# A two-block network on one core: the state space part over groups, its dt chain and the second rotary embedding rewritten

## What is computed

```python
# Mamba-2 mixer: 32 heads of 64, in 8 groups of 4 heads; state 128; 4 chunks of 128 tokens
z, xbc, dt_raw = split(h @ w_in)             # 2048 | 4096 | 32 columns
xbc = silu(causal_conv(xbc) + conv_b)        # -> xs (2048), B (8x128), C (8x128)
dt = softplus(dt_raw + dt_bias);  a = -exp(a_log)
a_cs = cumsum(dt * a)                        # inside each chunk
decay = exp(where(tril, a_cs[l] - a_cs[s], -inf))
y_diag = (C B^T * decay) @ (x * dt)
states = B^T @ (x * dt * exp(a_cs[last] - a_cs));  prev = scan(states, exp(a_cs[last]))
y = y_diag + (C @ prev) * exp(a_cs) + xs * d_skip
y = y * silu(z);  y = y * rsqrt(mean over the group of y^2 + eps) * norm_w
x = x + y @ w_out
# rotary embedding, on the first 32 of 128 dimensions of each head (6 key heads, 24 query heads)
out = concat([x1*cos - x2*sin, x2*cos + x1*sin, rest])     # x1, x2: 16 dimensions each
```

## Time and profile before

| | us |
|---|---|
| three runs: lowest, median, highest | 3761.51, 3762.31, 3772.96 |
| the profiled execution, its own time | 3773.22 |
| its span, first to last instruction | 3771.2 |
| TensorE busy | 3442.8 (91%) |
| VectorE, ScalarE, GpSimd busy | 1583.9, 881.0, 1646.8 |
| mean granted TensorE clock | 0.946 of 2.4 GHz |

### The profile page before, as it was taken

How to read it: one execution, slowest core, us unless ns; L and a number is a source line. 1 busy time by engine, 2 the same in 40 slices (tenths; PEclk the granted TensorE clock), 3 DMA queues, 4 the chain that set the end, 5 groups by cost and what they waited for, 6 DMA issues and landing times.

```text
span 3771.2 us, 43722 instructions
## 1 busy us (share of the span) xinstructions
PE 3442.8 (91%) x16384; PEld 2741.4 (73%) x16384; DVE 1583.9 (42%) x2525; ACT 881.0 (23%) x1473; POOL 1646.8 (44%) x872
## 2 busy tenths in 40 slices
PE   7998889999997999999899677899999986889998
PEld 4888768888995667888688344678887763777887
DVE  5877467522334742110224466343401117654321
ACT  3122231112533531100222133122201102432210
POOL 2430136657872034666466100356665540025664
PEclk9998999999999999999999777899999998999999
DMA  5520036524541012332232100123322211012331
GB/s 214 191 87 1 18 112 239 176 100 127 182 133 51 1 45 67 97 108 84 65 97 83 36 1 1 50 79 96 106 95 74 81 51 41 1 45 84 96 109 69
DMA packets 85172, 319.75 MB, mean 85 GB/s; under 512 B 9248, under 2 KB 11168, under 8 KB 84000
## 3 DMA queue, kind: packets, MB, share of 16 engines
q1 hardware_dynamic: 85024, 317.72, 25.4%
HBM read 315.59 MB, written 2.10 MB: 84 GB/s over the span
## 4 chain that ended last, share of the span: by engine, by line
PE 79%; DVE 10%; issue 4%; ACT 3%; POOL 2%; DMA 1%; SPq 0%; DVEq 0%; ACTq 0%; POOLq 0%
PE two L320 15%; PE two L319 15%; PE two L318 15%; PE two L443 7%; PE two L442 7%; PE two L441 7%; PE two L1784 2%; PE two L1762 2%; DVE small L1809 1%; PE two L2005 1%; PE two L1336 1%; POOL w_lo L275 1%; PE two L293 1%; PE two L1339 1%; PE two L294 1%
## 5 line engine op out<-in xcount | busy, mean ns | idle before, releaser
L318 PE MATMUL two<-h_hi,w_hi 128*128 128x512 f32 x2240 | 883.6, 394 | 25.4 <-POOL w_lo L275 25.4
L320 PE MATMUL two<-h_hi,w_lo 128*128 128x512 f32 x2240 | 887.8, 396 | 0.0
L319 PE MATMUL two<-h_lo,w_hi 128*128 128x512 f32 x2144 | 847.4, 395 | 0.0
L275 POOL TENSOR_TENSOR w_lo<-w_raw,w_hi 128x1024 fp32r<-128x1024 f32 x318 | 774.2, 2436 | 35.1 <-ACT w_hi L338 10.2
L273 POOL TENSOR_SCALAR w_hi<-w_raw 128x1024 fp32r<-128x1024 f32 x298 | 317.0, 1064 | 854.4 <-PE two L320 454.7
L420 POOL TENSOR_SCALAR w_hi<-w_raw 128x1408 fp32r<-128x1408 f32 (+1 forms) x106 | 133.3, 1257 | 1193.3 <-PE two L443 837.3
L318 PEld LDWEIGHTS two<-h_hi,w_hi 128*128 128x128 f32 x2240 | 424.5, 190 | 122.1 <-issue 24.9
L320 PEld LDWEIGHTS two<-h_hi,w_lo 128*128 128x128 f32 x2240 | 424.9, 190 | 91.7
L319 PEld LDWEIGHTS two<-h_lo,w_hi 128*128 128x128 f32 x2144 | 406.4, 190 | 92.9
L422 POOL TENSOR_TENSOR w_lo<-w_raw,w_hi 128x1408 fp32r<-128x1408 f32 (+1 forms) x112 | 339.3, 3031 | 10.5 <-ACT w_hi L478 1.7
L443 PE MATMUL two<-hid_hi,w_lo 128*128 128x512 f32 x704 | 277.3, 394 | 0.0
(11 more groups left out here) (431 smaller groups left out, 5548.3 us busy)
## 6 DMA issues: line engine op xcount, KB each, us to landing
w_raw<-w_f0u SPq DMA_DIRECT2D x88, 512.0 KB, 3.6
row_raw<-ada SPq DMA_DIRECT2D x48, 512.0 KB, 5.3
w_raw<-w_ssm SPq DMA_DIRECT2D x48, 512.0 KB, 3.5
w_raw<-w_f0d SPq DMA_DIRECT2D x32, 704.0 KB, 4.0
w_raw<-w_f1u SPq DMA_DIRECT2D x44, 512.0 KB, 3.5
w_raw<-w_f2u SPq DMA_DIRECT2D x44, 512.0 KB, 3.5
w_raw<-w_f3u SPq DMA_DIRECT2D x44, 512.0 KB, 3.5
ada_raw<-ada SPq DMA_DIRECT2D x32, 512.0 KB, 3.7
```

The costliest lines, as they stand in the source:

```text
L275: nc.gpsimd.tensor_tensor(s_lo[s][:, 0:self.kt], w_raw[j][:, 0:self.kt], s_hi[s][:, 0:self.kt].bitcast(f32), ALU.subtract).then_inc(split_ ...
L318: nc.tensor.matmul(dst, s_hi[s][:, k], hi, start=kk == 0, stop=False)
L319: nc.tensor.matmul(dst, s_hi[s][:, k], lo, start=False, stop=False)
L320: last = nc.tensor.matmul(dst, s_lo[s][:, k], hi, start=False, stop=kk == self.parts * self.kt - 1)
```

## The change

Three things.

**dt beside the `w_ssm` product.** `DtPart` is gone; `DtSide` puts the same steps after tiles of the z turns, now all written out (`peel=(1, 2, 3, 4)`). (0, 0) is the first tile of turn 0: ACT rounds `w_dt`, the identity and the mask. PE's product for dt follows (0, 3), as three f32r products per k. DVE clamps at (1, 0); ACT's exponential and DVE's whole series and running sums stand at (1, 1); ACT's two further exponentials and the pairs `cs_two`, `ec_two` (high part in partitions 0 to 31, remainder in 32 to 63) at (2, 2); PE's transposes at (3, 1), behind a wait for the DVE chain; the copies at (3, 3). The table of Silu is loaded again after each exponential. SP waits for `Apply` to be done at (0, 3) before it loads `w_dt` and the mask.

**One phase `Ssd` over all groups.** The row of a head is an f32r product of 64 rows (`sel` by `cs_two`), and a second f32r product (`ident_r` by `mask_r`) adds the mask in PSUM; ACT takes the exponential straight from PSUM with the token's own value as bias, four instructions of 128 columns per head. The DVE instructions L2013 are gone. The broadcast of exp(a_cs) is one f32r product per tile (`s_pair` by `ec_two`), `s_pair` being written by POOL once a group. The steps of neighbouring groups are interleaved: the sum, scaling and pair of group g-1 stand inside group g, rows and transposes of group g+1 inside the end of group g. All rows, broadcasts and sums share bank 3; the transposed x has only bank 2 for both halves. Ln and Exp come from one table, loaded once.

**The second rotary embedding in the evacuation.** `Rope` is not called for it. `RopeEvac` turns the first 32 partitions of a tile in PSUM: a DVE shuffle that swaps the halves, two multiplications, one addition; then ACT copies the tile. `RopeTables`, a phase ahead of the `w_kv` product, loads the two tables.

```diff
+        class RopeTables(Phase):
+            def sp(self, sp):
+                sp.wait_ge(*self.gate)
+                for name, dst in (("cos2", r2_cos), ("sin2", r2_sin)):
+                    a, w = CST[name]
+                    sp.dma_start(dst[:], cst[0:32, a:a + w]).then_inc(phase_in, 16)
+        class RopeEvac:
+            def dve(self, g, dve, i, a):
...
+                        dve.wait_ge(chunk_done, g.tile(i, n))
+                        nc.vector.stream_shuffle(w, v, SWAP).then_inc(self.swapped[0], 1)
+                        dve.wait_ge(self.swapped[0], self.swapped[1] + m + 1)
+                        nc.vector.tensor_tensor(v, v, r2_cos[:], ALU.mult).then_inc(self.turned[0], 1)
+                        nc.vector.tensor_tensor(t, w, r2_sin[:], ALU.mult).then_inc(self.turned[0], 1)
+                        dve.wait_ge(self.turned[0], self.turned[1] + 2 * m + 2)
+                        nc.vector.tensor_tensor(v, v, t, ALU.add).then_inc(self.roped[0], 1)
...
+            def pe(self, pe, i, n):
+                if (i, n) == (0, 3):
+                    pe.wait_ge(*upto(self.dtw_lo, 1))
+                    for k in range(ND):
+                        for q, (w_, h_) in enumerate(((dtw_hi, h_hi), (dtw_hi, h_lo), (dtw_lo, h_hi))):
+                            last = nc.tensor.matmul(ps[7][0:NSH, :], w_[:, k], h_[:, k], start=k == 0 and q == 0, stop=k == ND - 1 and q == 2)
+                    last.then_inc(self.dt_in_ps[0], 1)
+                if (i, n) == (3, 1):
+                    pe.wait_ge(*upto(self.dt_dve, 5))
...
+                def total(g):
+                    pe.wait_ge(*upto(self.sq, 2 * g + 2))
...
+                    for t in range(2):
+                        last = nc.tensor.matmul(ps[3][:], ones[:], s_out[t][:], start=t == 0, stop=t == 1)
+                    last.then_inc(self.sum[0], 1)
...
+                def exps(g, hh):
...
+                    for c in range(4):
+                        last = nc.scalar.activation(s_w[hh][:, c], ps[3][:, c * P:(c + 1) * P], ACT.Exp, bias=s_tok[:, 0, c, h:h + 1])
+                    last.then_inc(self.exp[0], 1)
...
+                    weight(g, 0)
+                    carry(g, 0)
+                    weight(g, 1)
+                    if g:
+                        scale(g - 1)
+                    carry(g, 1)
...
-        gm = Gemm(w_ssm, 48, 1, 8, hrhs, evac_act=sc.act, evac_dve=sc.dve, peel=(4,), gate_k=ap.tile_ready, table=ACT.Silu)
-        dt = DtPart(upto(sc.out, 32))
-        s = None
-        for g in range(NG):
-            s = Ssd(g, upto(s.y_tile, 2) if s else dt.done, dt.val)
+        dt = DtSide(ap.done)
+        gm = Gemm(w_ssm, 48, 1, 8, hrhs, evac_act=sc.act, evac_dve=sc.dve, peel=(1, 2, 3, 4), gate_k=ap.tile_ready, table=ACT.Silu, side=dt)
+        s = Ssd(upto(sc.out, 32), dt)
...
-        gm = Gemm(w_kv, 12, 1, 8, hrhs, evac_act=y_evac(kv), gate_k=ap.tile_ready)
+        rt = RopeTables(r.done)
+        re = RopeEvac(kv, 6, rt.val)
+        gm = Gemm(w_kv, 12, 1, 8, hrhs, evac_act=re.act, evac_dve=re.dve, gate_k=ap.tile_ready, peel=(1, 2))
...
-        rp = Rope([(kv[:, j], TL, None) for j in range(6)] + [(q2[:, j], TL, None) for j in range(24)], 2, gm.all_read, s_y)
```

More of the change, by code:

```diff
@@ L1874, in dve @@
                 if a < 4:
+                    for n in range(4):
+                        g.side.dve(dve, i, n)
                     return
@@ L1952, in dve @@
-            def dve(self, dve):
+                if (i, n) == (0, 0):
+                    act.wait_ge(phase_in, self.val)
+                    nc.scalar.copy(dtw_hi[:, :, :], dtw[:, :, :]).then_inc(self.dtw_hi[0], 1)
+                    nc.scalar.copy(ident_r[:], ident[:])
+                    nc.scalar.copy(mask_r[:], ssd_mask[:]).then_inc(self.mask[0], 1)
+                if (i, n) == (1, 1):
+                    act.wait_ge(*upto(self.dt_pos, 1))
+                    astep(nc.scalar.activation(d_t[0][:], ps[7][0:NSH, :], ACT.Abs, bias=bias))
+                    astep(nc.scalar.activation(d_t[0][:], d_t[0][:], ACT.Exp, scale=-1.0))
+                    a, w = VEC["a_log"]
+                    sig(nc.scalar, nc.scalar.activation(small[0:NSH, 48:49], vec[0:NSH, a:a + 1], ACT.Exp), self.dt_act)
+                    nc.scalar.preload_act_table(ACT.Silu)
@@ new lines, in act @@
+                if (i, n) == (2, 2):
+                    act.wait_ge(*upto(self.dt_dve, 3))
+                    sig(nc.scalar, nc.scalar.activation(d_ec[:], d_cs[:], ACT.Exp), self.dt_act)
+                    act.wait_ge(*upto(self.dt_dve, 4))
+                    sig(nc.scalar, nc.scalar.activation(d_t[0][:], d_t[0][:], ACT.Exp), self.dt_act)
+                    nc.scalar.preload_act_table(ACT.Silu)
+                    nc.scalar.copy(cs_two[0:NSH, :], d_cs[:]).then_inc(self.cs_hi[0], 1)
+                    nc.scalar.copy(ec_two[0:NSH, :], d_ec[:]).then_inc(self.cs_hi[0], 1)
@@ new lines, in y_tile, with pool @@
+            def y_tile(self, g, t):
+                return upto(self.y_step, 8 * g + 7 + t)
+            def pool(self, pool):
+                pool.wait_ge(*upto(self.dt.sel, 1))
+                for g in range(NG):
+                    pool.wait_ge(*upto(self.ec, 2 * g))
+                    nc.gpsimd.tensor_scalar(s_pair[:, :, :], sel[:, 4 * g:4 * g + 4].bitcast(f32).unsqueeze(2).to_broadcast([2 * NSH, 4, 64]), 1.0, 1.0,
+                                            ALU.mult, ALU.mult).then_inc(self.pair[0], 1)
```

547 lines of the change are left out of this document (318 added, 229 removed).

## The result

The changed kernel takes 3627.08 us, the median of four runs (3625.10 to 3628.96); the kernel before, run beside it, 3765.34 (3761.51 to 3772.96). The ratio is 0.9633, 95% interval 0.9615 to 0.9651: 138 us faster. The forecast was 3620 us, within 3595 to 3655.

What follows compares the result with a forecast made beforehand. PE holds 79% of the chain; the change targets three stretches outside its full-rate products, handoffs with no engine full. Terms -34.4 - 51.4 - 68.3 + 11 = -143.1 took 3773.2 to 3630.1 profiled, 3620 us as median; range 3595 to 3655.

Steps and rivals of the forecast that it cites:

- dt beside the product, -34.4: Between w_ssm product and state space part: 44.2 us removed, 5.5 and 1.3 of PE work and 3 of waiting added.
- the short end (31): DVE's dt chain beside POOL's splits: about 31 us if only two-input instructions are held; 41 was taken.
- The 3 us of waiting: In the w_ssm product: PE reaches its dt transposes at 55 us, its inputs come at about 58.
- The state space part, -51.4: All groups: first group 24.5, seven periods of 23.7 and end 13.5, together 203.9 us against 255.3.
- one fall a group: State space part: PE's clock falls to 1.2 GHz once per group, upon states and sum, adding 2.1 to 21.6 us.
- full clock: State space part, rival: PE at full clock in all groups, seven times 2.1 and some 3 us less, 3602; 12%.
- The 3 us for POOL's splits: End of the state space part: POOL's first two w_ssm_out splits come after the last s_pair and hold DVE.
- The rotary embedding, -68.3 and +11: Last w_q tile to Tokens: 72.0 us become 3.7; SP's wait for the norm delays w_kv by 11, between 8 and 15.
- Half clock throughout: State space part, rival: PE at half clock, period 27.5, 27 us more and 5 at the ends, 3652; 25%.
- SP's wait was not covered: Ahead of w_kv, rival: SP's wait is covered or costs under 3 us, 3610; 6%.
- The evacuation: w_kv and w_q tiles, rival: DVE's steps pass PE's 5.49 us and become the bound, over 3763; 2%.
- The part did pipeline: State space part, rival: the change does not pipeline, period at 30 again, 44 us more, 3664; 5%.

Runs made afterwards that it cites:

- the run on the kernel before: The kernel before with the rotary part of the change alone (no Rope phase, tables on SP after the norm): 3720.5 us, ratio 0.9879.
- dt alone: The changed kernel with the dt steps taken out of the w_ssm product and run behind it: 3653.1 us, ratio 0.9701.
- the early x dt: Changed kernel, tables early, sum before states, splits ahead, three unread products a group, next group's first x dt before the last y step: 3572.0 us.
- the three edits: The changed kernel with tables early, sum before the states and the first two w_ssm_out splits ahead of the state space part: 3573.4 us, ratio 0.9492.

## Why the prediction was right

**dt beside the product, -34.4.** Measured -37.2. The 6.8 us on PE came as 6.9. The step that failed is the chain's length. "If the 0.41 us instructions are held too, 14.7 / 2.03 = 7.2 tiles" gave DVE nothing to do in 3.46 of every 5.49 us. The rows show that instructions of both kinds are held, as I took it. But each of POOL's instructions held one DVE instruction at most, and that one was finished a quarter to half a microsecond after it; an instruction that DVE had begun was not broken off, and the reciprocal's 3.34 us passed beside two of POOL's instructions. So a tile of 5.49 us took 2.9 us of the chain (18.1 / 33.8 x 5.49), not 2.03, and the chain is 33.8 us, nearer to the short end (31) than to 41. The 3 us of waiting became 5.1 us of slack. The Trainium skill (GPSIMD Engine Reference, Specifications) names contention of GpSimd with VectorE's two-input instructions. The trace agrees that there is contention: 0.68 became up to 2.78. That entry gives no price, and the price decided this term.

**The state space part, -51.4.** Measured -49.9, with four terms that differ. The period: 23.9 against 23.7. The sum was right and its parts were not. DVE's work was taken at 17.6 with its gaps and is 15.4 us (neighbouring instructions overlap, two of 0.68 take 1.28, where I had added gaps); the waits were taken at about 6 and are 8.5, since the rounding (1.23) and the states (0.30) were not in the list and the one before `scale` is 4.20, close to the 4.4 that I gave for half clock. The two errors nearly cancel. The "DVE over 70% busy" that was to show it is 64%. The clock was right: one fall a group, upon states and sum (and already upon the transposes ahead of them), worth 2.3 us by the run with unread products, which reaches 21.64 where "at full clock throughout" gave 21.6. The first group: 27.5 against 24.5 (26.6 in the changed kernel's other trace). Its rows and exponentials take 2.75 us each where PE's clock is at half, against 2.4, and "10.3 to the last step" was 13.5: the states stand behind the last row, at half clock, and from the first broadcast to the last step it is 12.2 us. The end: 10.0 against 10.5 and 3. The 3 us for POOL's splits were right in size (2.8) and wrong in place: POOL's last `s_pair` is that of group 7, made in group 6, and the splits fall there. Three things changed in this part at once: DVE's four sets of instructions went, the rows became f32r products, and the order of the steps is new. No run takes them apart, so how the 49.9 us divide among them is not shown.

**The rotary embedding, -68.3 and +11.** Measured -68.4 and +10.8. The shuffle took 0.68 us for 32x512 in PSUM against 0.7. SP passed at 2777.83, chunk 0 was there at 2782.76, 4.08 us after its issue against 4.2. The run with early tables shows that the cost was this wait, and the run on the kernel before shows the two figures without the rest of the change. "Runs its first pair in about the time it took before" was not quite so: in the first 23 us of `w_kv` the granted clock was 0.73 against 0.86 before, and the first `w_q` product came 80.2 us after the first of `w_kv` instead of 78.0. Of the other traces with SP's wait some show these 2 us and some do not. That they are missing from the sum is luck: the tiles of `w_q` took 5.60 us in the trace of before and 5.49 in the changed kernel's, 2.2 us less, in code that PE has in common.

**The rivals.** In the order of the changed kernel full clock needs PE to be filled: 21.64 us a group came only with added products. Half clock throughout is out, the granted clock was 1.00 in the 8.9 us of broadcasts, heads and state product. (The two short stretches of the earlier trace rows show only the fall; the recovery that I read from them stands in the 4.3 us behind, 2155.7 to 2160.0, at 1.00.) SP's wait was not covered. The evacuation stood far from PE's 5.49 us with 2.9 on DVE. The part did pipeline.

**The sum.** For the profiled execution it gave 3630.1 us, and that took 3629.0: the start (+2.8), the dt steps (-2.8), the part (+1.5), the stretch to `w_kv` (-1.5) and the end (-0.7) leave -0.7 of the difference of -1.1 and cancel for the most part; the rest is tenths in the other rows and in the step from span to time. The start has no term in the forecast and nothing of the change in it, so its 2.8 us, which offset the dt steps, are chance. The 7 us between forecast and median come from a step outside the sum: I took off the 10.9 by which the profiled execution of before lay above its median, and the changed kernel's lies only 1.9 above.

## What to carry over

A stage that is moved beside a product needs its own length beside that product's helpers: here 18 us became 33.8, and only the place where it is collected, 5.1 us later, kept it free. In a loop whose engines hand over to each other, look for a step that an idle engine could have run: the squares were ready 2.7 us before PE began the states, and moving the sum up took out the wait and kept the clock, 4.2 to 5.5 us a group. And count the queue that a small load is put in front of: two tables, issued in 0.8 us, held the weight loads behind them for a norm, and PE with them for 10.8 us.

## What was not expected of the hardware

Unread products made the kernel faster: nine products of 512 columns, put where PE had 1.1 us of work in 3.5, raised the granted clock from 0.86 to 1.00 over a group and took 2.3 us off it.

With POOL, instructions of DVE that have two inputs and that have one input were both held, at most one for each of POOL's; the reciprocal of 32x512 passed two of POOL's instructions at its usual 3.34 us and they at theirs (1.05 and 2.41). Small work of POOL can be longer too: `s_pair` took 0.95 us in six groups of the changed kernel and 0.40 to 0.51 in the other two. That DVE holds it there is likely (at 2166.76 it starts together with DVE's weight) but no run tests it.

In many executions a whole product ran 2% slower at a granted clock of 1.00: its tiles took 5.60 us instead of 5.49. The kernel before does it too. In the trace of before it was `w_f0u` (42 tiles in a row) and `w_q` (21); with early tables `w_f2u` (41) and `w_q`; with dt alone and with the early x dt `w_f2u`; in the rotary run `w_f1u` (41), with the three edits that and `w_q`; in six traces nine or ten tiles of `w_ssm`. Of the thirteen traces only three have no such run of tiles: the changed kernel's first, the one with the sum first and the one with nine unread products a group. In the run with early tables the first products of `w_f2u` also stayed at the lower clock for longer (0.86 against 0.93 in the 48 us around its start), some 8 us together; with the tiles of `w_q` and some of `w_ssm` it hid the gain of 10.8 in that execution. So a part of the scatter between executions is this, and a difference of a few us between two medians tells little here. Its cause is open.
